# Six plain column tiles instead of five ahead of the paired products, and all weight low parts on VectorE, in a two-layer float32 decoder step

## What is computed

```python
def swiglu(x, w_gate, w_up, w_down):
    return (jax.nn.silu(x @ w_gate) * (x @ w_up)) @ w_down
x = x + 0.5 * rmsnorm(swiglu(rmsnorm(x, g[0]), ffn1_w_gate, ffn1_w_up, ffn1_w_down), g[1])
```

## Time and profile before

| | us |
|---|---|
| median of 3 runs | 2186.33 (2184.88 to 2187.07) |
| the profiled execution: its time | 2185.45 |
| its span, first to last instruction | 2183.5 |
| TensorE busy | 2109.8 (97%), 18816 matmuls |
| VectorE busy | 1342.1 (61%) |
| ScalarE busy | 1011.0 (46%) |
| GpSimd busy | 976.9 (45%) |
| DMA queue of SyncE | 33.5% of 16 engines |

### The profile page before, as it was taken

The page is one execution under the profiler, slowest core; times in us unless marked ns, Lnnn a source line. Parts: engine busy times, 40 slices in busy tenths (PEclk is TensorE's granted clock), DMA queues, the critical chain, the costliest instruction groups (busy, mean ns, idle before and its releaser), DMA issues.

```text
span 2183.5 us, 45630 instructions
## 1 busy us (share of the span) xinstructions
PE 2109.8 (97%) x18816; PEld 2055.8 (94%) x18816; DVE 1342.1 (61%) x2067; ACT 1011.0 (46%) x2059; POOL 976.9 (45%) x757
## 2 busy tenths in 40 slices
PE   8899999999999989999988999999999998999999
PEld 8899999999889979999988999999998898899998
DVE  5988601666357898851179885027654678988313
ACT  5466522534344546652254665235243545566422
POOL 3444574534324434454443445445342354444542
PEclk9899999999999999999998999999999999999999
DMA  6133343322233423343242334433223143233432
GB/s 185 53 101 99 116 121 91 85 71 68 60 90 102 128 66 104 98 126 97 78 136 64 102 98 128 112 83 84 70 64 98 55 117 114 78 102 97 132 91 78
DMA packets 395246, 209.80 MB, mean 96 GB/s; under 512 B 31920, under 2 KB 385472, under 8 KB 395040
## 3 DMA queue, kind: packets, MB, share of 16 engines
q1 hardware_dynamic: 394896, 206.84, 33.5%
q10 hardware_dynamic: 144, 0.06, 0.0%
HBM read 189.18 MB, written 17.67 MB: 95 GB/s over the span
## 4 chain that ended last, share of the span: by engine, by line
PE 82%; DVE 11%; ACT 2%; DMA 2%; issue 2%; POOL 1%; SPq 1%; DVEq 0%; ACTq 0%
PE ps L1024 44%; PE ps L1036 30%; PE ps L1304 1%; DMA w_raw<-in_ffn_w_gate 1%; DVE xn_lo L2232 1%; DVE stage L2406 1%; DVE x_ops L2427 1%; DVE numer L2844 1%; POOL w_lo L893 1%; DVE x_r L2429 1%; ACT w_hi L1646 1%; DVE x L2248 1%; DMA w_raw<-in_ffn_w_up 0%; DVE x_ops_f L2409 0%; DVE x_ops L2424 0%
## 5 line engine op out<-in xcount | busy, mean ns | idle before, releaser
L893 POOL TENSOR_TENSOR w_lo<-w_raw,w_hi 128x512 fp32r<-128x512 f32 (+1 forms) x424 | 560.2, 1331 | 759.6 <-ACT w_hi L1646 758.1
L1024 PE MATMUL ps<-xn_hi,w_hi 128*128 128x272 f32 x2368 | 549.1, 298 | 36.1 <-DVE gs L2385 18.4
L1646 ACT ACTIVATE w_hi<-w_raw 128x512 fp32r<-128x512 f32 (+1 forms) x424 | 254.4, 605 | 615.3 <-PE ps L1024 468.1
L1024 PE MATMUL ps<-xn_hi,w_lo 128*128 128x272 f32 x2368 | 531.3, 291 | 0.0
L1024 PE MATMUL ps<-xn_lo,w_hi 128*128 128x272 f32 x2368 | 530.8, 290 | 0.0
L1024 PEld LDWEIGHTS ps<-xn_hi,w_hi 128*128 128x128 f32 x2368 | 391.1, 191 | 59.2 <-DVE gs L2385 19.3
L1036 PE MATMUL ps<-x_ops,w_hi 128*128 128x272 f32 x2048 | 398.0, 291 | 1.5 <-ACT gs L1879 1.3
L1024 PEld LDWEIGHTS ps<-xn_lo,w_hi 128*128 128x128 f32 x2368 | 392.0, 191 | 0.3
L1024 PEld LDWEIGHTS ps<-xn_hi,w_lo 128*128 128x128 f32 x2368 | 390.2, 191 | 0.0
L1036 PEld LDWEIGHTS ps<-x_ops,w_hi 128*128 128x128 f32 x2048 | 325.2, 191 | 2.4 <-ACT gs L1879 2.3
L2214 DVE TENSOR_TENSOR acc<-acc,gs 128x544 f32<-128x544 f32 (+1 forms) x45 | 35.2, 783 | 319.5 <-ACT gs L1714 318.9
(11 more groups left out here) (401 smaller groups left out, 3799.3 us busy)
## 6 DMA issues: line engine op xcount, KB each, us to landing
w_raw<-in_ffn_w_down SPq DMA_DIRECT2D x160, 256.0 KB, 2.8
w_raw<-in_w_in SPq DMA_DIRECT2D x120, 256.0 KB, 2.8
w_raw<-in_ffn_w_gate SPq DMA_DIRECT2D x72, 256.0 KB, 2.9
spare_f<-in_ffn_w_gate SPq DMA_DIRECT2D x64, 256.0 KB, 2.9
spare_f<-in_ffn_w_up SPq DMA_DIRECT2D x64, 256.0 KB, 2.9
w_lo_f<-in_ffn_w_up SPq DMA_DIRECT2D x64, 256.0 KB, 2.9
w_raw<-in_ffn_w_up SPq DMA_DIRECT2D x40, 256.0 KB, 2.9
x_aside<-x SPq DMA_DIRECT2D x16, 544.0 KB, 4.8
```

What stands on the lines that cost most here:

```text
L893: pool.tensor_tensor(w_lo[:, q % RING, 0:m], w_raw[:, q % RAW, 0:m], w_hi[:, n % RING, 0:m].bitcast(F32), ALU.subtract).then_inc(w_split, 1)
L1024: mm = pe.matmul(pair(p)[:, a, :], w, z[:, half(a)], start=(k == 0 and j == 0), stop=(k == chunks - 1 and j == 2))
L1646: act.activation(w_hi[:, n % RING, 0:m], w_raw[:, q % RAW, 0:m], ACT.Copy).then_inc(w_hi_ready, 1)
```

## The change

One more of the 21 tiles is plain: PLAIN_TILES becomes 6 and PAIRS 15. BY_POOL becomes empty, so that VectorE makes all seven low parts of a pair. VectorE's queue between rstd and the pairs is reordered: x_lows(0) now stands between up(1) and gate(2), x_mix(1) behind gate(2), every later x_lows right behind a gate or an up, and w_mix(0) is cut in two halves ahead of and behind up(4). ScalarE's and GpSimd's queues are reordered to match, with tile 5 added. In `pair_step` the copy `keep(A11MINUS21)` moves ahead of the wait for first_sum and the first silu. As the number of pairs is odd now, the slots of even and odd pairs, their PSUM banks and their mixed buffers are exchanged, and the waits that guard them follow: w_mix(0) waits for the splits of the last two plain blocks (22 and 23) before it writes their raw slots, the third load of w_down waits for the third product of the last pair, and TensorE's first w_down tiles wait for other counts.

```diff
@@ -46,7 +46,7 @@
     RING, RAW = 6, 3
     DOWN_BLOCKS = -(-FC // 4)
 
-    PLAIN_TILES = 5
+    PLAIN_TILES = 6
     PAIRS = FC - PLAIN_TILES
     UP_PLAIN = 4 * PLAIN_TILES
     PRODUCTS = 7
@@ -78,7 +78,7 @@
     BLOCKS = B_DN2 + DOWN_BLOCKS * DC
     OPEN = 3
     PLAIN_BLOCKS = BLOCKS - 2 * PRODUCTS * PAIRS
-    assert (2 * PLAIN_TILES - 1) % 3 == 0 and PAIRS >= 4 and PAIRS % 2 == 0
+    assert PLAIN_TILES % 3 == 0 and PAIRS >= 3 and PAIRS % 2 == 1
 
     def plain(n):
 
@@ -320,7 +320,7 @@
                 return h_hi[:, t, :], h_lo[:, t, :]
             return xn_hi[:, t - EARLY_H, :], xn_lo[:, t - EARLY_H, :]
 
-        BY_POOL = (1, 4)
+        BY_POOL = ()
 
         def lows_to(done, k):
 
@@ -336,8 +336,8 @@
         def w_place(raws, lows, spares, w, k, after):
 
             if w % 2 == 0:
-                return raws[:, (after + (0 if k == 2 else 1)) % RAW, :] if k in (2, 6) else spares[k if k < 5 else 2][:]
-            return raws[:, (after + 2) % RAW, :] if k == 0 else lows[:, (after + k - 1) % RING, :]
+                return raws[:, (after + k) % RAW, :] if k in (1, 2) else spares[(0, None, None, 3, 4, 2, 1)[k]][:]
+            return raws[:, after % RAW, :] if k == 0 else lows[:, (after + k - 1) % RING, :]
 
         def w_sum(w, k, after):
 
@@ -347,9 +347,9 @@
 
             return w_place(w_raw_r, w_lo, spare, w, k, after)
 
-        ZS = (6, 3)
-        FIRST_COLS = (2, 4)
-        SECOND_COLS = (7, 5)
+        ZS = (6, 1)
+        FIRST_COLS = (0, 2)
+        SECOND_COLS = (7, 3)
 
         GAIN, BLR, HEAD, LOGIT = 0, DEPTH * 6 * DC, DEPTH * (6 * DC + 1), DEPTH * (6 * DC + 4)
 
@@ -589,7 +589,7 @@
             begun = [j for j in (B_DN1, B_DN2) if j <= i < j + RAW]
             if begun:
                 r = i - begun[0]
-                sp.wait_ge(w_used, l * BLOCKS + begun[0] - PRODUCTS * (2 - r // 2) + (2, 6, 0)[r] + 1)
+                sp.wait_ge(w_used, l * BLOCKS + begun[0] - PRODUCTS * (1 if r else 2) + r + 1)
             elif n >= RAW:
                 sp.wait_ge(w_split, q - RAW + 1)
             sp.dma_start(raw_view(w_raw[:, q % RAW, :], k1 - k0),
@@ -604,7 +604,7 @@
             if w >= 2:
                 sp.wait_ge(w_used, n0 + PRODUCTS * (w - 2) + k + 1)
             elif w == 1 and k == 0:
-                sp.wait_ge(w_split, after)
+                sp.wait_ge(w_split, after - 2)
             elif w == 1:
                 sp.wait_ge(w_used, n0 + k - RING)
             col = (PLAIN_TILES + w) * P
@@ -911,9 +911,12 @@
                 splits(n_up, n_up + 14)
                 low(0)
                 low(1)
-                splits(n_up + 14, n_up + 18)
+                splits(n_up + 14, n_up + 17)
                 low(2)
-                splits(n_up + 18, n_up + UP_PLAIN)
+                splits(n_up + 17, n_up + 21)
+                low(3)
+                splits(n_up + 21, n_up + UP_PLAIN)
+                low(4)
 
                 def w_lower(w, k):
                     n = n0 + n_up + UP_PLAIN + PRODUCTS * w + k
@@ -923,7 +926,6 @@
                     pool.tensor_tensor(w_slot(w, k, after), w_sum(w, k, after), w_hi[:, n % RING, :].bitcast(F32), ALU.subtract
                                        ).then_inc(w_low_pool, 1)
 
-                low(3)
                 for k in BY_POOL:
                     w_lower(0, k)
                 for t in range(PLAIN_TILES - 1, FC - 1):
@@ -1177,9 +1179,10 @@
                 product(A22, z)
             for t in range(DC - 1):
                 if t == 0:
+                    pe.wait_ge(h_scaled, f0 + FC - 1)
+                    pe.wait_ge(first_summed, PAIRS * (2 * l + which + 1))
+                elif t == 2:
                     pe.wait_ge(up_read, g0 + PLAIN_TILES)
-                elif t == 1:
-                    pe.wait_ge(h_scaled, f0 + FC)
                 elif t > 2:
                     pe.wait_ge(y_kept, y0 + t - 2)
                 for b in range(DOWN_BLOCKS):
@@ -1871,7 +1874,7 @@
 
                 n = n_up + UP_PLAIN + PRODUCTS * w
                 i = UP_PLAIN + PRODUCTS * w
-                mixed = (gs[:, 2, :], rstd[:])[w % 2]
+                mixed = (rstd[:], gs[:, 2, :])[w % 2]
                 z = ps[:, ZS[w % 2], 0:HT]
 
                 def keep(k, out, src):
@@ -1890,15 +1893,15 @@
                 keep(A22MINUS21, p_kept[:], ps[:, SECOND_COLS[w % 2], 0:HT])
                 high(i + 7)
                 if w == 0:
-                    act.wait_ge(h_ready, f0 + PLAIN_TILES - 2)
+                    act.wait_ge(h_scaled, f0 + PLAIN_TILES)
                 elif w == 1:
-                    act.wait_ge(h_scaled, f0 + PLAIN_TILES)
+                    act.wait_ge(h_ready, f0 + PLAIN_TILES)
                 keep(MIXED2, mixed[:, half(0)], z)
                 high(i + 8)
                 high(i + 9)
+                keep(A11MINUS21, mixed[:, half(1)], z)
                 act.wait_ge(first_summed, pairs0 + w + 1)
                 act.activation(gs[:, w % 2, half(0)], gs[:, w % 2, half(0)], ACT.Silu).then_inc(silu_kept, 1)
-                keep(A11MINUS21, mixed[:, half(1)], z)
                 high(i + 10)
                 high(i + 11)
 
@@ -1909,24 +1912,30 @@
             h_high(0)
             h_high(1)
             high(14)
+            silu(2)
             high(15)
             act_x_operands(act, l, which, 1)
             high(16)
-            silu(2)
+            h_high(2)
             high(17)
-            h_high(2)
             act_x_operands(act, l, which, 2)
             high(18)
+            silu(3)
             high(19)
-            silu(3)
             high(20)
+            h_high(3)
+            high(21)
             act_x_operands(act, l, which, 3)
-            high(21)
-            h_high(3)
             high(22)
+            silu(4)
             high(23)
-            silu(4)
             high(24)
+            h_high(4)
+            high(25)
+            high(26)
+            silu(5)
+            high(27)
+            high(28)
             for w in range(PAIRS):
                 pair_step(w)
             second_silu(PAIRS - 1)
@@ -2429,7 +2438,7 @@
                 dve.tensor_tensor(x_r[:, c:DC:4, HT:T], x[:, c:DC:4, half(1)], x_r[:, c:DC:4, 0:HT].bitcast(F32), ALU.subtract
                                   ).then_inc(x_op_ready, 2)
 
-            def w_mix(w):
+            def w_mix(w, parts=(0, 1)):
                 n = n_up + UP_PLAIN + PRODUCTS * w
                 slot = [w_sum(w, k, after) for k in range(PRODUCTS)]
                 mixed0 = 4 * (pairs0 + w)
@@ -2437,21 +2446,29 @@
                 def arrived(j):
                     dve.wait_ge(q_arrived[w % 2][j], arrivals(l, which, w))
 
+                if 0 in parts:
+                    w_mix_first(w, n, slot, arrived)
+                if 1 in parts:
+                    w_mix_second(w, n, slot, mixed0)
+
+            def w_mix_first(w, n, slot, arrived):
                 arrived(0)
-                if w:
+                if w == 0:
+                    dve.wait_ge(w_split, after - 1)
+                else:
                     dve.wait_ge(w_used, n - 2 * PRODUCTS + 1 + 1 if w > 1 else n - PRODUCTS + 1 - RING)
                 dve.tensor_tensor(slot[1], slot[0], slot[4], ALU.add).then_inc(w_mixed, 1)
                 arrived(1)
                 dve.tensor_tensor(slot[4], slot[4], slot[5], ALU.add).then_inc(w_mixed, 1)
+
+            def w_mix_second(w, n, slot, mixed0):
                 if w == 0:
-                    dve.wait_ge(w_split, after - 2)
+                    dve.wait_ge(w_split, after)
                 else:
                     dve.wait_ge(w_used, n - 2 * PRODUCTS + 2 + 1 if w > 1 else n - PRODUCTS + 2 - RING)
                 dve.wait_ge(w_mixed, mixed0 + 1)
                 dve.tensor_tensor(slot[2], slot[1], slot[5], ALU.add).then_inc(w_mixed, 1)
-                if w == 0:
-                    dve.wait_ge(w_split, after - 1)
-                else:
+                if w:
                     dve.wait_ge(w_used, n - 2 * PRODUCTS + 6 + 1 if w > 1 else n - PRODUCTS + 6 - RING)
                 dve.wait_ge(w_mixed, mixed0 + 3)
                 dve.tensor_tensor(slot[6], slot[2], slot[3], ALU.add).then_inc(w_mixed, 1)
@@ -2471,7 +2488,7 @@
                 dve.tensor_tensor(g, g, ps[:, FIRST_COLS[w % 2], 0:HT], ALU.add).then_inc(first_summed, 1)
 
             def second_sum(w, a):
-                u = (gs[:, 2, :], rstd[:])[w % 2][:, half(a)]
+                u = (rstd[:], gs[:, 2, :])[w % 2][:, half(a)]
                 if a:
                     dve.wait_ge(z_kept, 4 * (pairs0 + w) + 4)
                     dve.tensor_tensor(u, u, p_kept[:], ALU.add).then_inc(second_summed, 1)
@@ -2481,7 +2498,7 @@
 
             def combine(w):
                 g = gs[:, w % 2, :]
-                u = (gs[:, 2, :], rstd[:])[w % 2]
+                u = (rstd[:], gs[:, 2, :])[w % 2]
                 dve.wait_ge(silu_kept, 2 * (pairs0 + w) + 2)
                 dve.wait_ge(second_summed, 2 * (pairs0 + w) + 2)
```

(15 more changed lines are left out.)

## The result

| | before | after |
|---|---|---|
| median of the timed runs, same chip | 2185.61 us (2184.57 to 2187.07) | 2164.36 us (2163.39 to 2166.59) |
| profiled execution | 2185.45 us | 2166.59 us |
| granted TensorE clock over the span | 0.984 | 0.992 |

The ratio is 0.9904, with a 95% interval of 0.9887 to 0.9921: 21.3 us less, where 20.3 were forecast.

The account below looks back on a forecast made before the run. VectorE's queue, not TensorE, was taken to set T1: 63.0 - 57.55 - 10.52 = -5.1 us per FFN, -20.3 for four, giving 2166.0 us as a median; range 2147 to 2180.

Parts of the forecast that it names:

- Parts 1 and 2: Start of each FFN: 12 more matmuls (6.0 us if nothing else moved); VectorE's queue 7.24 + 27.64 + 15.9 = 50.8 us to T0.
- T0: End of VectorE's low part (0,0), for the first pair of an FFN; forecast at R + 50.8 us.
- R: VectorE's first gate scaling in an FFN, the zero from which the forecast counts its times.
- T1: First matmul of an FFN's second pair; forecast at T0 + 12.2 = R + 63.0 us.
- Rival (b): Start: the waits only move, fifteen GpSimd operations at 1.28 us, T1 near R + 66.5, -1.6 per FFN, 2180 us; chance 0.22.
- Rival (a): Start: TensorE becomes the bound, added splits cost VectorE nothing, T1 = R + 55.3, -12.8 per FFN, 2135 us; chance 0.12.
- The waits on the way: TensorE's waits between gate 3 and the first pair: 0.7 us for gate(2), about 4 at up 4; first pair near R + 48.5.
- Part 3: T0 to T1: MIXED2's copy 4.4 us after T0 where wanted at 3.0, five products 7.5, third copy 0.3: 12.2 us.
- Part 4: Steady pairs: two more low parts on VectorE, 9.3 + 1.2 - 0.76 = 9.7 of 10.52 us, so no cost.
- the old 0.55 us: TensorE's wait before the change ahead of the first pair's last product, for the third copy queued behind the silu.
- Rival (c): Steady pairs: VectorE cannot hold the pair time, each 1.2 us longer, +52 us, 2238; decides from 0.34 per pair; chance 0.07.

## Why the prediction was right, and where it was not

**The start (Parts 1 and 2)** held. T0 was put at R + 50.8 and measured R + 50.65, with the 15 GpSimd operations assumed; T1 at R + 63.0, measured 63.3 in all four FFNs. Four more VectorE operations moved T1 by their own length, which shows the mechanism. The price of 1.06 us per GpSimd operation, taken from nine of them in the trace of before, comes out again in the trace of after: 43.40 us from up(1) to T0 less 27.64 of work are 15.76 for 15 operations, 1.05 each. It also stood up in a direct measurement (0.98 from ten taken away). Rival (b), 1.28 us each, has fallen with that, and so has the whole-length reading of the Trainium skill (SBUF — State Buffer, SBUF: two separate sides) as a price: the trace agrees that the two engines hold each other up, not that each operation costs its full length. Rival (a), in which the added splits cost VectorE nothing, fell too. (Rival (b)'s own terms add up to R + 66.3, not 66.5, and 2179 us; nothing hangs on it.)

**The waits on the way.** Up 3 was to wait 0.7 us: none in the third FFN, 0.81 in the first. Up 4 about 4 us: 3.58. TensorE at the first pair near R + 48.5: R + 49.2 in the third FFN (1170.07 less the wait of 1.78) and about the same in the fourth. In the first and second it is R + 50.7, and the wait for low part (0,0) only 0.25 us. There the clock did fall behind the wait at up 4 (see the last section), and from up 4 to the first pair TensorE took 19.8 us instead of 18.3: 1.5 us, where 1.8 had been allowed. So the 2.3 us that the prediction left between TensorE and T0 were 1.8 in two FFNs and 0.25 in the other two, where one more wait on the way would have moved T1.

**T0 to T1 (Part 3)** was put at 12.2 us and came out at 12.6, the difference between 63.0 and 63.3 with 0.15 off at T0. MIXED2 waits 0.92 where 1.4 were worked out.

**The sum.** T1 - R grew by 63.28 - 57.60 = 5.68 us less the pair of 10.52: -4.84 per FFN, -19.4 for four, where -20.3 stood. The profiled executions differ by 18.9, the medians by 21.3; the 2 us between these are as much as single executions of one kernel differ.

**Where a step failed: Part 4, and the copy in Part 3.** "No cost, TensorE's products cover it" was argued from VectorE's busy share in a pair (9.7 of 10.52 us). The conclusion was right for the whole change, but not for that reason: with the copy behind the silu the same low parts cost 34 us in the kernel before and 35 in the pairs of the kernel after, at a VectorE busy share of 89 and 88%. And "the copy's move is worth the old 0.55 us" mis-sized it by far. Alone it gives 1.7 us, but within the change its absence costs 45. Rival (c) had the right threat (a pair that becomes longer, deciding from 0.34 us) and the wrong place: it lay neither in the idle slot nor in the stretched row but in the number of low parts ahead of first_sum, with no slack in the chain to TensorE's last product. The trace of before showed it: the copy ended 0.05 us ahead of the weight load that it gates. Had the diff lacked that one moved line, the same working would have given about 2166, and 2210 would have been measured. That part of the forecast was right by luck.

**Which part made the gain.** By runs, each against the kernel before beside it: the copy 1.7 us; all low parts on VectorE on top of it 5.2 (6.9 for both); the sixth tile and the orders the other 14.4. How these 14.4 divide between tile and orders is not shown: the order alone gave nothing, and the run with the tile and three of VectorE's operations at their old places is held up by ScalarE's queue. Nor is it shown how much of the gain is TensorE's clock, which in the first pair is at 1.00 now and was at 0.75 to 0.86 behind the last x operand before. These don't add up freely: in the whole change the two low parts on GpSimd make no difference. The Trainium skill (Perfetto Trace Analysis, Optimizing Scalar/DVE Operations) warns that moving work between these two engines might not help; in the steady pairs the trace agrees (2164.43 against 2164.36 us), in the start it does not, where ten subtractions moved to VectorE gave most of 13.4 us.

Left open: how much of the 13.4 us is the cast order's, of which only one execution was timed.

## What to carry to other kernels

An engine's busy share doesn't say whether it can take one more instruction: follow the chain of in-order queues to the work that must not stop, and look at how far ahead of it the last link ends; 0.05 us of slack at 89% busy made 0.60 us cost 34. Where one queue sets the end, a wait that is removed on another engine only moves, and new work for that other engine is free up to the queue's end (here with 0.25 us to spare in two of four FFNs). When an experiment puts back one engine's old order, look whether the other engines' queues still fit it. Price an instruction by what it does to the critical queue: on GpSimd these cost VectorE's queue 1.0 us each, on VectorE 0.60.
